# Sixteen low parts of weight blocks in each layer's GLA heads: written by GpSimd in place of VectorE

## What is computed

```
x = x + 0.5 * _swiglu(_rmsnorm(x, p['norm_ffn1']), p['w_ffn1_in'], p['w_ffn1_out'])
xn = _rmsnorm(x, p['norm_mix'])
(mq, mk, mv, mo, mg_if, gq, gk, gv, gg, glr, lx, ly, mgate) = _split_cols(xn @ p['w_in'])
...
merged = gm[:, :, 0] * y_ml + gm[:, :, 1] * y_gla + gm[:, :, 2] * y_lru
x = x + merged.astype(x.dtype) @ p['w_out']
x = x + 0.5 * _swiglu(_rmsnorm(x, p['norm_ffn2']), p['w_ffn2_in'], p['w_ffn2_out'])
```

```
b = jnp.cumsum(ac, axis=2)
diff = jnp.where(causal[:, :, None], b[:, :, :, None, :] - b[:, :, None, :, :], -jnp.inf)
A = jnp.einsum('bhtd,bhsd,bhtsd->bhts', qc, kc, jnp.exp(diff))
o = jnp.einsum('bhts,bhsv->bhtv', A, vc) + jnp.einsum('bhtd,bhdv->bhtv', qc * jnp.exp(b), S)
```

## Time and profile before

| | |
|---|---|
| median of 3 runs | 3126.54 us (3124.81 to 3127.68) |
| the profiled execution | 3129.91 us, its span 3128.1 us |
| TensorE matmul busy | 3055.7 us, 98% of the span |
| VectorE busy | 1902.3 us, 61% |
| ScalarE busy | 1038.8 us, 33% |
| GpSimd busy | 12.9 us |
| all low parts of weight blocks (L1154) | 248 instructions, 525.8 us, mean 2120 ns |

### The profile page before, as it was taken

How to read it: one execution, slowest core, us unless ns; L and a number is a source line. 1 busy time by engine, 2 the same in 40 slices (tenths; PEclk the granted TensorE clock), 3 DMA queues, 4 the chain that set the end, 5 groups by cost and what they waited for, 6 DMA issues and landing times.

```text
span 3128.1 us, 60370 instructions
## 1 busy us (share of the span) xinstructions
PE 3055.7 (98%) x25824; PEld 3013.2 (96%) x25824; DVE 1902.3 (61%) x2705; ACT 1038.8 (33%) x992; POOL 12.9 (0%) x36
## 2 busy tenths in 40 slices
PE   7999999999999999999999999999999999999998
PEld 7999999999999999999999999999999999999997
DVE  5434467778887874434454344776888788643344
ACT  3222232334344642212232122333334355421212
POOL 1000000000000000000000000000000000000000
PEclk9999999999999999999999999999999999999999
DMA  4222233233222222222222222233222322222222
GB/s 145 74 99 89 72 112 109 106 110 110 96 100 88 74 83 94 78 97 75 87 94 81 101 89 84 94 125 129 94 89 95 96 91 74 96 81 83 92 79 71
DMA packets 51916, 292.18 MB, mean 93 GB/s; under 512 B 9385, under 2 KB 12265, under 8 KB 23881
## 3 DMA queue, kind: packets, MB, share of 16 engines
q1 hardware_dynamic: 37152, 241.43, 22.3%
q10 hardware_dynamic: 13984, 48.48, 4.2%
q0 software_dynamic: 656, 0.52, 0.1%
HBM read 268.90 MB, written 21.50 MB: 93 GB/s over the span
## 4 chain that ended last, share of the span: by engine, by line
PE 84%; DVE 9%; ACT 4%; issue 2%; DMA 1%; ACTq 0%; DVEq 0%; POOL 0%; POOLq 0%
PE stream_b L415 36%; PE stream_a L415 35%; PE stream_a L502 4%; DVE wl L1154 1%; DVE xc L1653 1%; ACT wh L836 1%; PE stream_b L508 1%; PE mix L622 1%; PE mix L562 1%; PE mix L723 1%; PE mix L543 1%; PE mix L625 1%; ACT L1059 0%; PE mix L555 0%; PE mix L698 0%
## 5 line engine op out<-in xcount | busy, mean ns | idle before, releaser
L836 ACT ACTIVATE wh<-stage 128x2048 fp32r<-128x2048 f32 (+2 forms) x246 | 435.8, 1772 | 773.9 <-PE stream_b L415 561.3
L1154 DVE TENSOR_TENSOR wl<-stage,wh 128x2048 fp32r<-128x2048 f32 (+2 forms) x248 | 525.8, 2120 | 112.2 <-ACT wh L836 88.4
L415 PE MATMUL stream_a<-xh,wh 128*128 128x272 f32 x2560 | 537.5, 291 | 27.0 <-DVE xl L1160 13.0
L415 PE MATMUL stream_b<-xh,wh 128*128 128x272 f32 x2560 | 538.3, 291 | 2.1 <-issue 1.2
L415 PE MATMUL stream_a<-xl,wh 128*128 128x272 f32 x2560 | 531.3, 289 | 0.0
L415 PE MATMUL stream_b<-xl,wh 128*128 128x272 f32 x2560 | 531.3, 289 | 0.0
L415 PE MATMUL stream_a<-xh,wl 128*128 128x272 f32 x2560 | 529.8, 288 | 0.0
L415 PE MATMUL stream_b<-xh,wl 128*128 128x272 f32 x2560 | 529.7, 288 | 0.0
L415 PEld LDWEIGHTS stream_a<-xh,wh 128*128 128x128 f32 x2560 | 404.6, 189 | 31.3 <-DVE wl L1154 13.0
L415 PEld LDWEIGHTS stream_b<-xh,wh 128*128 128x128 f32 x2560 | 405.4, 189 | 8.4 <-issue 3.7
L415 PEld LDWEIGHTS stream_b<-xh,wl 128*128 128x128 f32 x2560 | 404.1, 189 | 1.0 <-issue 1.0
(11 more groups left out here) (349 smaller groups left out, 4360.9 us busy)
## 6 DMA issues: line engine op xcount, KB each, us to landing
stage<-in_w_mix SPq DMA_DIRECT2D x88, 1024.0 KB, 4.8
stage<-in_w_up SPq DMA_DIRECT2D x87, 1024.0 KB, 4.8
stage<-in_w_down SPq DMA_DIRECT2D x32, 768.0 KB, 4.2
stage<-in_w_down SPq DMA_DIRECT2D x32, 640.0 KB, 3.9
CS<-in_c ACTq DMA_DIRECT2D x8, 1024.0 KB, 4.7
out_o_sc<-CS ACTq DMA_DIRECT2D x8, 1024.0 KB
CS<-in_s ACTq DMA_DIRECT2D x8, 1024.0 KB, 4.8
out_o_ss<-CS ACTq DMA_DIRECT2D x8, 1024.0 KB
```

Of the source, the lines that this page charges most:

```text
L415: mm = [pe.matmul(out(h), a(h), b(h), start=f, stop=z) for h in range(2)]
L836: act.activation(wh[:, slot, 0:width], stage[:, slot, 0:width], ACT.Copy).then_inc(hi_done, 1)
L1154: tt_(wl[:, slot, 0:width], stage[:, slot, 0:width], wh[:, slot, 0:width].bitcast(F32), ALU.subtract).then_inc(split_done, 1)
```

## The change

The sixteen blocks of each layer whose low part stood in VectorE's `gla_head` (blocks n+2 to n+5 of each of the four heads, so the last two are the first blocks of the LRU stage) get it from GpSimd, in a loop of its own after the `xs` copies. Each waits for the high part of its own block and for the low part of the block before. The four `split_lo` calls leave VectorE's `gla_head`. VectorE gets one wait, after the first LRU tile, for the last of the sixteen; its next low part then follows in the count.

```diff
--- before.py
+++ after.py
@@ -402,6 +402,12 @@
                 ins.then_inc(xs_ready, 1)
+                for b in range(HEADS * HEAD_BLOCKS):
+                    n = L * LAYER_BLOCKS + BLK_MIX + HEADS * HEAD_BLOCKS + 2 + b
+                    pool.wait_ge(hi_done, n + 1)
+                    pool.wait_ge(split_done, n + 2)
+                    pool.tensor_tensor(wl[:, b % 2, :], stage[:, b % 2, :], wh[:, b % 2, :].bitcast(F32),
+                                       ALU.subtract).then_inc(split_done, 1)
@@ -1529,7 +1535,6 @@
                 take(t + 1, 1, kT[:])
-                split_lo(n + 2, 0, 2 * D)
                 if not first:
@@ -1547,7 +1552,6 @@
                 dve.memset(t8[:], 0.0).then_inc(b_fac, 1)
-                split_lo(n + 3, 1, 2 * D)
                 take_gate(L, i, t + 4, 0, 0, acts, "silu", None)
@@ -1593,7 +1597,6 @@
                     states(c, DV, lambda c_: eb[:, c_ * C + C - 1:(c_ + 1) * C], lambda c_: c_, b_u, b_c, B * NC)
-                split_lo(n + 4, 0, 2 * D)
                 masked_keys(Kf[0:NS], None if last else lambda: take_decays(L, i + 1, 2)).then_inc(b_keys, 1)
@@ -1611,7 +1614,6 @@
                           between=None if last else lambda: sum_decays(L, i + 1))
-                split_lo(n + 5, 1, 2 * D)
                 sample_states(eb, 3, 2, b_us, B, number)
@@ -1751,6 +1753,7 @@
                 lru_x(L, 0, 0, 0)
+                dve.wait_ge(split_done, L * LAYER_BLOCKS + (BLK_MIX + 2 * HEADS * HEAD_BLOCKS + 4))
                 invert_root(L * (2 * HEADS) + (2 * HEADS - 1))
```

## The result

The changed kernel takes 3185.0 us (median of 4 runs, 3182.8 to 3187.3) against 3125.7 before: a ratio of 1.0194, 95% interval 1.0181 to 1.0207. It is slower by 59 us. The forecast was 3190.

What follows compares the result with a forecast made beforehand. TensorE, 98% busy, bounds the kernel. 59 (`b_fac`) + 3 (state reads) + 7 (clock) - 6 ("issue") + 1 (LRU) = +64 us, 3129.9 to 3194 profiled; the median is 3.4 lower: 3190. Range 3122 to 3204.

Steps and rivals of the forecast that it cites:

- Length on GpSimd: Each added GpSimd subtraction of 128 x 2048 takes 4.6 us, between limits of 2.5 and 4.9.
- Exclusion for a whole instruction: A two-input VectorE instruction and a GpSimd instruction reading SBUF exclude each other throughout; basis of the forecast, chance 0.42.
- Low parts late but in time, new wait of VectorE free: GpSimd's lateness is hidden; at the LRU start VectorE's wait before the reciprocal costs nothing, low part ready about 952.1 to 953.3.
- `b_fac` 7.6 us late in the third head: Collisions delay the third head's flag to 856.4; less the slack of 0.7, TensorE waits 7 us.
- rival 1: Exclusion, but only one of two collisions ahead of `b_fac` happens in each head: 3162 us, chance 0.18.
- The second collision: Third head, block n+3: GpSimd holds 846.2 to 850.8, after six products; alone it means 3.3 us of wait.
- Where TensorE pauses: At `b_fac` in all eight GLA heads, near 7 us each; 2 x (9.1 + 3 x 6.8) = 59 us.
- The term for the clock: After new pauses the granted clock falls and a tile takes 1.4 us more, in about five heads: 7 us.
- State reads: Block n+4's collision delays the decay inputs; TensorE's state reads wait 0.6 us in six heads, say 3 us.
- "Issue": TensorE's unexplained waits amid the score products, 9.1 us before; 6 us may vanish during long `b_fac` waits.
- Rivals 2 and 3: GpSimd kept out by VectorE's runs or sharing at half rate: 3130, chance 0.17; no effect on each other: 3124, chance 0.18.
- Rival 4: LRU stage paced by its start, so 2.2 us removed before the reciprocal moves on in both layers: 3119 us, chance 0.05.

Runs made afterwards that it cites:

- the reordering: Kernel before, all low parts on VectorE; in LRU the next pair's first tile goes ahead of the last low part, ScalarE's last high part earlier: 3109.6 us, ratio 0.9940.
- the kernel with only n+3: Changed kernel with only block n+3's low part on GpSimd, the other three of each head back on VectorE: 3167.0 us, ratio 1.0132.

## Why the prediction was right

- **TensorE bounds, VectorE's freed time is worth nothing.** Right: 4.4 us a head freed without collisions moved nothing beyond the interval.
- **Length on GpSimd.** 4.6 us by interpolation (2048 x 2.17 ns + 0.1 is 4.5, which I had put down as 4.6); undisturbed ones took 4.53 to 4.68. The 1.0 ns of the second read was a choice between two values, so part of this fit is luck. The group's mean of 4.94 has waiting in it.
- **Exclusion for a whole instruction.** Right, and shown alone: useless work of GpSimd that reads costs 111 to 122 us, useless writing some 7 (one run each), the low parts gated away from two-input instructions nothing. It fits that reads of PSUM by VectorE go on beside GpSimd.
- **Low parts late but in time, new wait of VectorE free.** Right. At the LRU start VectorE waited 2.08 us for the last low part and began the reciprocal here:

```profile
983.52 3.55 DVE L1393 RECIPROCAL hsq<-hsq 128x544 f32<-128x544 f32 x1 [2.08 <-issue]
```

GpSimd's last low part ended at 983.44. TensorE is behind the heads 30.2 us later than before by then (974.37 against 944.15), which puts the 953.42 of the earlier trace rows at 983.6; its wait for `xc` went from 2.7 to 2.9.

- **`b_fac` 7.6 us late in the third head.** The head began at 817.81 before and 836.88 after; the flag came 31.0 and 37.5 us behind that, so 6.6 late. The 1.0 us too many lies ahead of `b_diff`, which was 5.4 late, not 6.3: `Hh` made the differences start 1.1 us late and not 1.4, `kh` stood 4.3 us more and not 4.6, and the forecast's rounding added 0.3. GpSimd did not get in within the fourteen differences but behind them, as rival 1 has it; `kh` stood there in their place, so this changed nothing. The second collision came as said, 3.4 us.
- **Where TensorE pauses.** This was wrong. The sum put 59 us on `b_fac`, and the sign named for it, a wait near 7 us in all eight heads, did not come: it is 14.9 us in seven, 4.0 at most. The forecast's list of meeting points left out the value copy, which in the third head has less slack than the flag (0.05 us at most against 0.7), though its own step for the third head has the copy end at 847.4 in place of 843.16. The delay is met there, ahead of the gate tile, with +21, and at the flag with +12.5; with +4.2 for k in the first heads, 38 us. The term for the clock was too small in turn: 7 us forecast, matmuls busy 21 us longer. Pause and slow tile use up what would have been wait at the flag: in the third head the tile took 9.0 us and next to no wait was left, in the second it ran at full clock and the wait for the flag was 3.1 us. So the two errors nearly cancel, and not by luck: in seven of the eight heads TensorE still waits for the flag, which then sets the head's length however the time before it is filled. Heads two to four grew by 7.3, 6.4 and 4.8 us (6.8 forecast), the first by 10.8 (9.1 and the clock).
- **State reads.** 0.6 us each forecast, 0.2 measured; together 1.3.
- **"Issue".** 6 us off forecast, 1.8 found.

So +64 forecast stands against +56 in span of the profiled executions and +59 in the medians. The eight heads grew by 56.3 us (29.2 in the first layer, 27.1 in the second), and the forecast's terms for them (59 + 3 + 7 - 6) make 63: the 7 us too many are of the size of the 1.0 us by which the third head's flag was put too late, taken for six heads; the other heads were not taken apart in this way. Rivals 2 and 3 fell with the first stretched row. Rival 4's chain in the LRU stage exists, as the reordering showed, but this change doesn't reach it.

Open: when GpSimd gets in. In the kernel with only n+3 it entered once inside an unbroken run of VectorE's and once was held off for two instructions, after its wait had been met alike; in the two kernels with useless reading it entered a run after 0.4 us in one and was held off for 3.0 us in the other. No run here settles what decides it. Rival 1 rests on it; ahead of `b_diff` it would have cost as much as the forecast, since `kh` comes right behind the run.

## What to carry to other kernels

Before work goes to GpSimd, read what VectorE runs at that moment: instructions with two inputs in the on-chip memory, and copies within it, stand for GpSimd's whole instruction, while those from PSUM and the reciprocal run on. The price is GpSimd's length at each collision, paid on the path if a flag lies behind; a wait on GpSimd that moves it past the flag, or shorter instructions, take most of it back. List every point at which the bounding engine meets the other, with its slack: the one left out here, the value copy, was the tightest in the third head. And freeing an engine of 71 us gains nothing when no one waits for it.

## What was not expected of the hardware

- A one-input copy of 32 columns, 0.18 us before, stood 4.41 us (`Qm`).
- GpSimd's memsets stretch VectorE's one-input casts (0.57 to 1.99 us) and leave two-input subtractions alone.
- GpSimd's row begins when its wait is met, not when it gets in: 5.87 us for an instruction of 4.6, and 6.22 for a copy of 3.4.
- With a pause of 3.1 us ahead of it, the matmuls of the gate tile come two every 0.45 us in place of 0.25 for the first 5.6 us (865.5 to 871.1), at a granted clock of 0.50; with one of 2.8 us, in the second head, all come at full clock.
